# Head of layer 0 of a two-layer trunk: conditioning products ahead of the turnings, turnings between the first projection's columns, rotation tables in fewer passes

## The reference, cut to what matters

```python
mod = (jax.nn.silu(c) @ ada_w[layer] + ada_b[layer])[:, None, :]
sh_m, sc_m, g_m, sh_f, sc_f, g_f = jnp.split(mod, 6, axis=-1)
h = _modulate(x, norm_g[layer, 0], sh_m, sc_m)     # rmsnorm(x) * g * (1 + sc_m) + sh_m
u = h @ w_in                                       # 1024 columns: 512 pooling, 512 S5
# S5: per group g of 16 channels, 64 complex states p
step = exp(log_step); lr = min(lam_re, -1e-4); mag = exp(lr * step)
ar, ai = mag * cos(lam_im * step), mag * sin(lam_im * step)
bbr, bbi = f * (b_re, b_im)                        # complex factor f of lam and step
x_t = a * x_(t-1) + bb @ u_t                       # complex recurrence over the 256 tokens
y = Re(c @ x) + d_skip * u;  y = gelu(y);  y * sigmoid(y @ w_glu)
```

## Time and profile before

| | |
|---|---|
| time, median of 3 runs | 1631.36 us (1627.72 to 1631.84) |
| profiled execution: span from first to last instruction | 1626.4 us (no other time of that execution is given) |
| TensorE matmul busy | 1535.8 us, 94% of the span |
| VectorE busy | 408.2 us, 25% |
| ScalarE busy | 219.9 us, 14% |
| GpSimd busy | 91.2 us, 6% |
| HBM read | 486.97 MB |

### The profile page before, as it was taken

The page is one execution under the profiler, slowest core; times in us unless marked ns, Lnnn a source line. Parts: engine busy times, 40 slices in busy tenths (PEclk is TensorE's granted clock), DMA queues, the critical chain, the costliest instruction groups (busy, mean ns, idle before and its releaser), DMA issues.

```text
span 1626.4 us, 23976 instructions
## 1 busy us (share of the span) xinstructions
PE 1535.8 (94%) x10645; PEld 895.8 (55%) x10646; DVE 408.2 (25%) x858; ACT 219.9 (14%) x431; POOL 91.2 (6%) x106
## 2 busy tenths in 40 slices
PE   8999999999999999989999998999899989998986
PEld 6676587777588855444443353356666643433322
DVE  5794213232245555221000001020010020100102
ACT  3422200000321144220000000000000000000001
POOL 6153000000000012000000000000000000000000
PEclk9999999999999999998999999999999999999999
DMA  9567467664563425368999986999999969999996
GB/s 343 205 238 284 164 251 258 239 225 158 191 249 116 163 93 199 124 237 333 414 414 414 366 285 262 416 416 412 411 408 404 393 240 413 414 416 412 414 417 241
DMA packets 160084, 490.01 MB, mean 301 GB/s; under 512 B 15888, under 2 KB 18896, under 8 KB 147664
## 3 DMA queue, kind: packets, MB, share of 16 engines
q1 hardware_dynamic: 153024, 482.52, 76.7%
q10 hardware_dynamic: 6928, 5.56, 1.2%
HBM read 486.97 MB, written 1.08 MB: 300 GB/s over the span
## 4 chain that ended last, share of the span: by engine, by line
PE 81%; DMA 6%; issue 2%; DVE 1%; ACT 0%; SPq 0%; DVEq 0%
PE bank L1821 28%; PE bank L1340 20%; PE bank L1857 13%; PE bank L1557 5%; DMA ring<-in_moe_w_down 5%; PE bank L1666 3%; PE bank L1731 3%; PE bank L1793 2%; DMA arena<-in_moe_w_gate 1%; PE bank L1838 1%; PE bank L1681 1%; PE bank L1365 0%; PE bank L1389 0%; PE bank L1354 0%; PE bank L1347 0%
## 5 line engine op out<-in xcount | busy, mean ns | idle before, releaser
L1821 PE MATMUL bank<-ring,arena 128*32 128x256 f32 (+3 forms) x3376 | 345.7, 425 | 31.4 <-issue 25.2
L1340 PE MATMUL bank<-arena,ring 128*128 128x256 f32 x1264 | 280.3, 381 | 1.4 <-ACT arena L698 1.1
L1821 PEld LDWEIGHTS bank<-ring,arena 128*32 128x32 f32 (+1 forms) x3376 | 159.9, 120 | 208.9 <-issue 160.3
L1340 PEld LDWEIGHTS bank<-arena,ring 128*128 128x128 f32 x1264 | 238.6, 191 | 34.0 <-ACT arena L698 1.5
L1857 PE MATMUL bank<-ring,arena 128*32 128x256 f32 (+1 forms) x1568 | 191.6, 463 | 12.1 <-DMA ring<-in_moe_w_down 11.2
L1259 DVE TENSOR_TENSOR arena<-arena,bank 128x512 f32<-128x512 f32 (+2 forms) x44 | 24.4, 577 | 639.0 <-PE bank L1821 639.0
L1821 PE MATMUL bank<-arena 128*32 128x256 f32 (+3 forms) x1488 | 158.5, 424 | 6.6 <-issue 3.4
L1857 PEld LDWEIGHTS bank<-ring,arena 128*32 128x32 f32 (+1 forms) x1568 | 74.8, 120 | 120.0 <-issue 80.1
L1821 PEld LDWEIGHTS bank<-arena 128*32 128x32 f32 (+1 forms) x1488 | 73.9, 121 | 84.9 <-issue 55.9
L837 ACT ACTIVATE arena<-bank 128x512 f32<-128x512 f32 (+2 forms) x44 | 21.1, 508 | 630.2 <-PE bank L1838 536.5
L1557 PE MATMUL bank<-ring,arena 128*128 128x512 f32 x176 | 76.7, 594 | 1.5 <-PE bank L1340 1.5
(11 more groups left out here) (280 smaller groups left out, 1168.7 us busy)
## 6 DMA issues: line engine op xcount, KB each, us to landing
ring<-in_moe_w_down SPq DMA_DIRECT2D x86, 1024.0 KB, 16.9
ring<-in_moe_w_gate SPq DMA_DIRECT2D x82, 1024.0 KB, 16.7
ring<-in_moe_w_up SPq DMA_DIRECT2D x70, 1024.0 KB, 18.2
ring<-in_ada_w SPq DMA_DIRECT2D x24, 2048.0 KB, 9.1
arena<-in_moe_w_up SPq DMA_DIRECT2D x42, 1024.0 KB, 16.9
arena<-in_moe_w_gate SPq DMA_DIRECT2D x30, 1024.0 KB, 19.0
arena<-in_moe_w_down SPq DMA_DIRECT2D x26, 1024.0 KB, 16.1
ring<-in_m_w_in SPq DMA_DIRECT2D x12, 2048.0 KB, 8.7
```

What stands on the lines that cost most here:

```text
L1340: ins = mm(out_, l, r, start=i == 0, stop=i == len(pairs) - 1, **kw)
L1821: ins = mm(ps[base + b // per][m * h:m * h + m, w * (b % per):w * (b % per) + w], hcur3[:, kc, m * b:m * b + m], sl[:, kc - half * rows, w ...
```

## The change

Five things are done. (1) TensorE: turn_x(1) moves up to behind ada_turn(0), in the place of one group of six stay_warm products; ada_mm(3) directly follows ada_turn(2); only b_turn 0 and 1 stand behind it. (2) TensorE: b_turn 2 to 7 stand in pairs between the four column products of mixin 1, all in banks 6 and 7, and none in the S5 loop. (3) ScalarE: the copies bt_copy and the third conditioning copy follow that order; bt_copy 4 to 7 stand behind the first half of the sines. (4) VectorE: the first pass of a table quarter becomes four passes of 128x256 with a per-partition factor, and the comparison pass goes; the cosine's angle is now the absolute value of the sine's. (5) ScalarE takes the cosine as the sine of a quarter turn minus that, with the constant from a small tile set in the beginning.

```diff
--- before.py
+++ after.py
@@ -143,7 +143,7 @@
         stat = sb("stat", [P, 16])
         rst = sb("rst", [P, 10])
         s5_tmp = sb("s5_tmp", [P, TOK])
-        eps = sb("eps", [P, 1])
+        eps, quarter_turn = sb("eps", [P, 1]), sb("quarter_turn", [P, 1])
         dtw = sb("dtw", [P, KC, HEADS])
         rw = sb("rw", [P, KC, NE])
         rwg = cT[:, :, 0:NE]
@@ -635,7 +635,7 @@
                     c.inc(f(dst[:, HALF * h:HALF * h + HALF], ps[base + h][:, :], ACT.Copy), "grow_ready")
 
 
-            act.wait_ge(s["cT_zero"], 2)
+            act.wait_ge(s["cT_zero"], 3)
             act.wait_ge(s["x_dec_in"], 16)
             squares(0)
             act.wait_ge(s["cols_ready"], 1)
@@ -653,22 +653,29 @@
 
             def bt_copy(i):
                 act.wait_ge(s["b_turned"], i + 1)
-                c.inc(f(bt[:, 2 * i:2 * i + 2], bank((4 if i < 4 else 6) + i % 2, 2, 2, P), ACT.Copy), "bt_ready")
+                c.inc(f(bt[:, 2 * i:2 * i + 2], bank((4 if i < 2 else 6) + i % 2, 2, 2, P), ACT.Copy), "bt_ready")
             ada(1)
             ada(2)
-            for i in range(4):
+            ada(3)
+            for i in range(2):
                 bt_copy(i)
-            ada(3)
             hT_high(1, 1, mod[:, 0, 0])
+            for i in range(2, 4):
+                bt_copy(i)
 
             def table_sines(half):
                 act.wait_ge(s["tab_ready"], half + 1)
                 qs = slice(half * NQ // 2, (half + 1) * NQ // 2)
                 for k in range(2):
-                    c.inc(f(tables[:, k, qs], tables[:, k, qs], ACT.Sin, scale=TWO_PI), "tab_sin")
+                    if k:
+                        c.inc(f(tables[:, 1, qs], tables[:, 1, qs], ACT.Sin, bias=quarter_turn[:, 0:1], scale=-TWO_PI), "tab_sin")
+                    else:
+                        c.inc(f(tables[:, 0, qs], tables[:, 0, qs], ACT.Sin, scale=TWO_PI), "tab_sin")
             table_sines(0)
             act.wait_ge(s["band_ready"], 6)
             for h in range(2):
+                for i in range(4 + 2 * h, 6 + 2 * h):
+                    bt_copy(i)
                 act.wait_ge(s["u_mm"], h + 1)
                 c.inc(f(uT[:, 2 * h:2 * h + 2], bank(4 + h, 2, TOK), ACT.Copy), "u_ready")
             act.wait_ge(s["c_turned"], 1)
@@ -680,8 +687,6 @@
                         src = bank(i, 4, P)[64 * h:64 * h + 64, :, at:at + 16]
                         dst = ct[64 * h:64 * h + 64, j:NQ:4, i, at:at + 16]
                         c.inc(f(dst, src, ACT.Copy), "ct_ready")
-            for i in range(4, 8):
-                bt_copy(i)
             table_sines(1)
 
             def pool_to_sbuf(i):
@@ -951,6 +956,7 @@
 
             c.inc(v.memset(cT[:, :, :], 0.0), "cT_zero")
             c.inc(v.memset(eps[:, :], EPS), "cT_zero")
+            c.inc(v.memset(quarter_turn[:, :], TWO_PI / 4), "cT_zero")
             dve.wait_ge(s["rows_turned"], 1)
             c.then(v.tensor_copy(cols[:, :, :], bank(0, 3, P)), "cols_ready")
             c.then(ts(prm[:, LR], lam_re, -1e-4, None, ALU.min), step)
@@ -1001,12 +1007,12 @@
             def table_turns(quarter):
                 qs = slice(quarter * NQ // 4, (quarter + 1) * NQ // 4)
                 tS, tC = tables[:, 0, qs], tables[:, 1, qs]
-                c.then(tt(tS, t_row.unsqueeze(1).broadcast_to([P, NQ // 4, TOK]),
-                          prm[:, TAU, qs].unsqueeze(2).broadcast_to([P, NQ // 4, TOK]), ALU.mult), step)
+                for q in range(quarter * NQ // 4, (quarter + 1) * NQ // 4):
+                    c.inc(ts(tables[:, 0, q], t_row, prm[:, TAU, q:q + 1], None, ALU.mult), step)
+                dve.wait_ge(s[step], c.n[step])
                 c.then(ts(tC, tS, ROUND, -ROUND, ALU.add, ALU.add), step)
                 c.then(tt(tS, tS, tC, ALU.subtract), step)
-                c.then(ts(tC, tS, 0.25, None, ALU.is_gt), step)
-                c.inc(stt(tC, tS, 0.25, tC, ALU.add, ALU.subtract), "tab_ready" if quarter % 2 else step)
+                c.inc(stt(tC, tS, -1.0, tS, ALU.mult, ALU.max), "tab_ready" if quarter % 2 else step)
             table_turns(0)
             mods(0, 4)
             scale_cols(1, 1, mod[:, 0, 1], norm_col(0, 0))
@@ -1404,33 +1410,37 @@
 
                 if i == 0:
                     pe.wait_ge(s["bx_ready"], 8)
-                if i == 4:
+                if i == 2:
                     pe.wait_ge(s["mod_ready"], 1)
-                if i >= 2:
+                if i >= 4:
                     pe.wait_ge(s["bt_ready"], i - 1)
                 for k in range(4):
-                    ins = turn(ps[(4 if i < 4 else 6) + i % 2][:, P * k:P * k + P], bx[:, k % 2, 2 * i + k // 2], ident[:, :])
+                    ins = turn(ps[(4 if i < 2 else 6) + i % 2][:, P * k:P * k + P], bx[:, k % 2, 2 * i + k // 2], ident[:, :])
                 ins.then_inc(s["b_turned"], 1)
             for i in range(3):
                 ada_mm(i)
                 ada_turn(i)
-                if i < 2:
+                if i == 0:
+                    pe.wait_ge(s["cols_ready"], 1)
+                    turn_x(1)
+                if i == 1:
                     stay_warm(WARM_ADA, 5)
-            for i in range(4):
-                b_turn(i)
             ada_mm(3)
-            pe.wait_ge(s["cols_ready"], 1)
-            turn_x(1)
+            b_turn(0)
+            b_turn(1)
             ada_turn(3)
 
             w = slot(arrived(AT["mixin", 1]), KC, HALF)
-            pe.wait_ge(s["bt_ready"], 4)
+            pe.wait_ge(s["bt_ready"], 2)
             for m in range(4):
                 pairs = [(w[:, kc, P * m:P * m + P], hT[:, kc]) for kc in range(KC)]
                 dst = ps[4 + m // 2][:, TOK * (m % 2):TOK * (m % 2) + TOK]
                 ins = chain(dst, pairs) if m else first_chain(dst, pairs, 1)
                 if m % 2:
                     ins.then_inc(s["u_mm"], 1)
+                if m < 3:
+                    b_turn(2 * m + 2)
+                    b_turn(2 * m + 3)
             pe.wait_ge(s["u_mm"], 2)
             pe.sem_inc(s["tile_used"], 1)
             pe.wait_ge(s["c_in"], 64)
@@ -1479,7 +1489,7 @@
 
                 if q >= 2:
                     pe.wait_ge(s["bu_used"], 2 * (q - 1))
-                if q >= 8:
+                if q >= 4:
                     pe.wait_ge(s["bt_ready"], q // 2 + 1)
                 for k in range(2):
                     ins = mm(ps[2 + q % 2][:, TOK * k:TOK * k + TOK], bt[:, q, k], uT[:, q // 4], start=True, stop=True)
@@ -1488,9 +1498,6 @@
             for q in range(NQ):
                 if q + 1 < NQ:
                     s5_in(q + 1)
-                if q == 0:
-                    for i in range(4, 8):
-                        b_turn(i)
                 if q - 1 in ADA_AT:
                     ada_turn(ADA_AT[q - 1])
                 if q >= 2:
```

## The result

| | before | after |
|---|---|---|
| median | 1629.86 us (4 runs, 1627.72 to 1631.84) | 1646.96 us (4 runs, 1644.41 to 1647.14) |
| profiled span | 1626.4 us | 1645.0 us |
| mean granted clock | 0.987 | 0.978 |

The ratio is 1.0100, 95% interval 1.0079 to 1.0122: the change makes the kernel 1% slower, some 16 us. That lies well outside the range of 1625.0 to 1632.2.

What follows compares the result with a forecast made beforehand. TensorE, 81% of the chain of waits, was taken to bound the kernel. Columns starting 4.0 us earlier, less 1.0 us up to the fourth S5 input product, gave 3.0 us: 1628.4 us, range 1625.0 to 1632.2.

Steps and rivals of the forecast that it cites:

- What bounds the kernel now: Whole kernel: TensorE is 81% of the chain of waits, transfers 6%; a microsecond won in the head should reach the end.
- The head: Work up to the fourth S5 input product: 4.0 us won less 1.0 us lost, 3.0 us earlier.
- When the columns start: Head, ahead of the column products: turnings removed before them let them start at 39.0 instead of 43.01, 4.0 us earlier.
- rival A: Conditioning products: the clock falls in their new order, columns start at 41.3, 1.1 us slower than before, 1632.5; chance 0.09.
- T0: Start of the column products on TensorE: 43.01 in the earlier trace, forecast 39.0.
- From T0 to the fourth S5 input product: Columns and S5 loop: moved turnings net 0.43 us later, plus 0.6 us of new wait; 35.0 us instead of 34.02.
- the copies of C: Pooling product: it waits for ScalarE's 16 copies, until now hidden by the b_turns; 0.6 us of new wait.
- The loop: S5 loop: two engines near full, no edit touches its work, its end at a fixed distance from its fourth input product.
- Rival B: Loop or expert stage: the gain is given back there, net 0, 1631.4 us; chance 0.13.
- Beside the path: VectorE's table quarters: 2.5 to 3.5 us saved in all, worth nothing; cosine bias and new memset also nothing.
- The range: Median of the whole kernel: 1625.0 to 1632.2 us, with cases A to C and the spread of a median.

Runs made afterwards that it cites:

- e2: Kernel before with six stay_warm products removed and 7 waits added, so TensorE's program is as long as after's: 1645.53 us, ratio 1.0092.
- e13: Kernel before with an unused 4-byte tile directly ahead of arena, so arena alone starts 32 bytes further: 1632.31 us, ratio 1.0028.
- e5: Kernel before with an unused 4-byte tile behind eps, every tile from dtw to arena 32 bytes further, no instruction different: 1633.12 us, ratio 1.0032.
- e3: Kernel before with the table edit alone (short passes, no comparison, cosine with quarter_turn), TensorE's program as long as before: 1635.68 us, ratio 1.0039.
- e9: Kernel before with an unused tile of 128 bytes a partition behind eps: 1634.81 us, ratio 1.0041.
- e6: Kernel before with two unused tiles behind eps, all tiles from dtw on 64 bytes further: 1637.50 us, ratio 1.0052.
- e7: Kernel after with 43 added waits restoring TensorE's program length and quarter_turn declared behind arena: 1626.56 us, ratio 0.9990 of before.
- e1: Kernel after with 43 waits (21 instructions) behind the last S5 output product, restoring TensorE's program length: 1633.46 us, ratio 1.0023 of before.
- e4: Kernel after with the six stay_warm products kept, TensorE's program 3 instructions longer than before: 1630.94 us, ratio 1.0014 of before.
- e8: Kernel after with the six stay_warm products kept (as e4) and quarter_turn declared behind arena: 1626.05 us, ratio 0.9992 of before.
- e12: Kernel of e8 with 95 more waits (47 instructions) in TensorE's program: 1637.57 us, ratio 1.0051 of before.
- e17: Kernel of e8 with 128 unused bytes ahead of ring and 128 behind eps: 1622.36 us, ratio 0.9945 of before.
- e16: Kernel before with 128 unused bytes ahead of ring and 128 behind eps, both ring and arena on multiples of 256: 1624.95 us, ratio 0.9971.
- e11: Kernel before with 471 waits (235 instructions) added to TensorE's program ahead of the wait for ys_ready: 1670.70 us, ratio 1.0255.

## Why the prediction was wrong

**What bounds the kernel now: the step that failed.** Of the expert weights the prediction says: "that part starts later or earlier with the work ahead of it and keeps its length. A microsecond won in the head should therefore reach the end." The head's microsecond did reach the experts (-0.92 at 825 us), but that part didn't keep its length. An item's start hangs on TensorE's own program too: the gap behind the branch ends some 1.5 us behind the landing of a fetch of instructions (at the first place, in before and after), and the earlier trace rows had 2% of the chain as "issue", which I read over. And its transfers hang on where ring and arena stand (409, 414 or 419 GB/s). Both were changed by edits that I had costed at nothing: the move of turn_x, with which six stay_warm products go, and the tile of 4 bytes for the quarter turn.

What was mis-sized, in terms of before's 1629 us: code position, forecast 0, measured 15.0 us (e2). The start of arena, forecast 0 ("The new memset stands at 1.2 us, before anybody waits: nothing."), measured 4.6 to 6.4 us for after's 32 bytes (e13, e5, e3; e9 and e6, at 128 and 64 bytes, have 6.7 and 8.5). The head, forecast -3.0, measured -1.6 (e7). Together 18 to 20; after is 16.3 us slower, with an interval of 12.9 to 19.9. Whether the two losses overlap (while TensorE waits for its program, weights arrive) can't be told within these intervals.

**When the columns start.** Forecast 39.0, range 38.1 to 39.95; it was 40.86. In after's trace the clock was 0.50 from 20 to 33 us, and products 1 and 2 ran in 3.64 and 3.13 us. That is the time of rival A, which had T0 at 41.3. Its extra 1.8 us in the first column product did not come (3.69 us, as in the earlier trace rows). But rival A's cause, turnings where stay_warm products stood, is not shown. e1 has after's instructions up to there, and its clock is 1.00 from 12 to 34 us. e5 has before's instructions, with all stay_warm products, and its clock is at 0.50 from 21 to 33. The timelines of e1, then of e5:
```profile
21.70 1.92 PE L1371 MATMUL bank<-ring,cT 128*32 128x512 f32 x16 [0.95 <-DMA ring<-in_ada_w]
...
39.40 3.69 PE L1360 MATMUL bank<-arena,ring 128*128 128x256 f32 x16 [1.14 <-DVE arena L918]
```
```profile
21.75 3.64 PE L1366 MATMUL bank<-ring,cT 128*32 128x512 f32 x16 [1.42 <-DMA ring<-in_ada_w]
...
45.46 3.69 PE L1355 MATMUL bank<-arena,ring 128*128 128x256 f32 x16 [1.14 <-DVE arena L914]
```
So after's late T0 is a fall of the clock that comes in one trace and not in another of the same instructions, and what sets it stays open. The sixteen turnings start at 18.71 in after and the clock is at 0.50 over 20 to 21; in e1 they start at 18.81 and it is 1.00.

The forecast's sums call a granted clock of 1.00 the upper level and one of 0.50 the lower; in before it came back at 38.1 (0.72 over 38.0 to 38.2, 1.00 over 38.2 to 38.4). At 0.50 the conditioning product took 3.64 us in after, where the sum had 3.84. That the clock would be back before 38.1, with the product in place of turnings, was an estimate, and 39.0 was the middle that it led to; no run shows that this order is what brings it back. The clock was back by 36 in e7 (0.55 over 34 to 36, 1.00 over 36 to 38), but in e3 too, which has before's order (0.51, then 1.00).

The forecast's T0 came in the other two traces of the new head, 39.40 in e1 and 38.92 in e7, where product 3 waits for its transfer as I had it. With the stay_warm products kept it is 37.76 to 39.44 (e4, e8, e12, e17); in e8 the landing of mixin 1, which I had as no hindrance at 37.5, is the last to come (1.56 us). The 43.01 that I started from is one draw as well: the eleven other kernels with before's order on TensorE have 41.00 to 45.46, at the median 41.5. Most of them run the first column product in 5.38 instead of 3.69 us, and their last S5 output product comes at 145.0 at the median, against 144.87 in before. So the head's gain is better read there: 1.1 us in after, 1.3 in e7 and 2.5 in e1, e4 and e8.

**From T0 to the fourth S5 input product.** Forecast 35.0, measured 35.07; the wait for the copies of C was 0.47 instead of 0.6, and the three pairs of turnings take 0.9 us each without a wait. It is 35.07 in e1 as well, but 36.8 in e7 and e8, whose first column product ran partly at the lower clock (0.80 and 0.67 over 38 to 40) and took 5.4 us.

**The loop.** Rival B's first half, that the loop gives the gain back, was wrong. The fourth input product is 1.10 us earlier and the last output product 1.09. Its second half pointed at the expert stage, but priced it at nothing gained, not at a loss.

**Beside the path.** A table quarter took 4.38 us (32.38 to 36.76), forecast 4.2 to 4.6, and nobody waited for it. VectorE's first S5 step waits 4.79 us for the input product:
```profile
59.75 1.42 DVE L1039 TENSOR_TENSOR arena<-bank,ring 128x512 f32<-128x512 f32 x2 [4.79 <-PE bank L1495]
```

**The range.** It was made of the head's uncertainties alone, with 0.05 for slower. No term stood for what an edit does to code and tiles that it doesn't touch.

## What to carry to other kernels

An edit that adds or removes instructions ahead of data-dependent branches moves every later branch target, and one that adds a tile moves every later tile: compare kernels with both restored before reading a difference of 1% as the edit's. Tiles that receive large transfers are worth placing first, on multiples of 256 bytes; here that gave 0.3% for two unused tiles (e16). Where the chain of waits shows "issue" behind a branch, look for packets of the instruction queue in it: here they were fetches of the program, and one gap went from 2.15 to 7.17 us by a shift of 21 instructions. A start time read from one trace is one draw where the clock falls in some executions: kernels with the same order had 41.00 to 45.46.

## What the runs showed of the hardware

- A branch into an expert item costs TensorE 0.8 to 5.5 us in before. The longest, 4.98 and 5.49 us, come at a DMA share of 0.15 and 0.13, those of 3.19 and 2.15 at 1.03, so full weight queues don't set the length. With the same code 21 instructions earlier (after, e2) a second wait of 4.65 us follows after two products at the second item, and at the fifth the gap is 7.17 instead of 2.15 us. -21 and +235 instructions (e2, e11), 256 apart, give the same gaps within 0.3 us. Where the stretches end was inferred, not measured, and e12 shows that the account isn't complete.
- Packets of 4096 bytes of the weight queue take 159 ns at the median if ring and arena start on multiples of 256 bytes (e16, e17), and 162 to 164 in most two-microsecond slices of e5, where neither does; over 1080 to 1160 us, with both on such a start, arena alone and neither the core moved 419, 414 and 409 GB/s (e16; before; e5).
- 471 waits on a count long reached took 25 us (e11), 107 ns for each of the 235 instructions that they compile to; 95 took 5.2 us (e12), 110 ns for each of 47; 43 of them in e1 cost 0.4 us, in a place where the next product waits for ScalarE 1.09 us anyway.
- In the head the clock differs between kernels with the same instructions there. With the new head it is 1.00 from 12 to 34 us in e1 and 0.50 from 20 to 33 in after; with before's it is 1.00 from 12 to 40 in e13 and 0.50 from 21 to 33 in e5. T0 is 39.40 and 40.86, 41.00 and 45.46. I didn't settle what sets it.
